# Top-k masks computed between projection tiles, output transposes one place later, one convolution tap on ScalarE

## The reference

```python
gdn_out = gdn_mixer(g_qkv, ...)      # gated delta rule, chunks of 64, 4 heads; output normed and gated
att = dsa_attend(...)                # scores of an indexer, the top 256 (or T // 4) keys of a query, softmax over them
ssm_out = ssd_mixer(s_z, s_xbc, ...) # state space scan
x = x + gate1 * (concat([gdn_out, att, ssm_out]) @ w_out)
```

```python
y = sum(ext[:, j:j + T] * w[j] for j in range(4))
_, sel = lax.top_k(score, topk)      # ties to the lower index
o = o * rsqrt(mean(o * o) + EPS) * norm_g * silu(gate)
```

## Time and profile before

| | |
|---|---|
| median of 3 runs | 4491.47 us (4491.46 to 4493.82) |
| profiled execution, its own time | 4497.23 us |
| its span | 4495.4 us |
| mean granted TensorE clock | 0.947 |
| TensorE busy, share of the span | 91% |
| VectorE, ScalarE | 50%, 23% |

### The profile page before, as it was taken

One profiled execution on the slowest core, in us unless ns is written; L12 is line 12 of the kernel. 1 busy time (PEld: TensorE's weight loads), 2 busy tenths in 40 slices (PEclk: granted clock), 3 DMA queues, 4 the chain that ended last, 5 costly groups with the idle time before them and its releaser, 6 DMA issues.

```text
span 4495.4 us, 54493 instructions
## 1 busy us (share of the span) xinstructions
PE 4086.0 (91%) x21348; PEld 2293.8 (51%) x21348; DVE 2255.5 (50%) x4568; ACT 1029.1 (23%) x2145; POOL 68.8 (2%) x128
## 2 busy tenths in 40 slices
PE   5999888688989999999989998977889799999996
PEld 2545554457545555545545455544575455554553
DVE  3246566655344445454542565565562444444445
ACT  2134444234210000000021344442350100000001
POOL 0000000000000000000000000000000000000000
PEclk8999999789989999999999999987999899999998
DMA  4124111123121322121121121111231111111211
GB/s 196 47 101 149 45 50 38 62 100 123 34 86 66 113 97 92 38 80 38 39 92 58 44 69 50 56 65 57 83 120 40 70 41 45 38 38 38 80 33 56
DMA packets 112880, 311.28 MB, mean 69 GB/s; under 512 B 9456, under 2 KB 57264, under 8 KB 104816
## 3 DMA queue, kind: packets, MB, share of 16 engines
q1 hardware_dynamic: 101392, 253.06, 16.2%
q0 software_dynamic: 10368, 40.58, 2.3%
q10 hardware_dynamic: 864, 14.16, 0.7%
HBM read 253.03 MB, written 54.47 MB: 68 GB/s over the span
## 4 chain that ended last, share of the span: by engine, by line
PE 83%; DVE 8%; DVEq 3%; ACT 2%; issue 2%; ACTq 1%; DMA 1%; SPq 0%; POOL 0%; POOLq 0%
PE PS L1287 34%; PE PS L803 15%; PE PS L1280 6%; PE PS L1328 3%; PE PS L783 2%; DVE big L1793 2%; DVE hT L1793 2%; PE PS L1364 2%; PE PS L1216 2%; PE PS L905 1%; PE PS L731 1%; PE PS L1236 1%; PE PS L970 1%; DVE big L1790 1%; PE PS L981 1%
## 5 line engine op out<-in xcount | busy, mean ns | idle before, releaser
L803 PE MATMUL PS<-hT,ring 128*128 128x512 f32 (+1 forms) x2304 | 844.6, 512 | 0.0
L803 PEld LDWEIGHTS PS<-hT,ring 128*128 128x128 f32 x2304 | 372.5, 196 | 318.3 <-issue 306.8
L1287 PE MATMUL PS<-hT,ring 128*128 128x512 f32 x832 | 372.4, 600 | 16.8 <-ACTq L1430 10.4
L1287 PE MATMUL PS<-xT 128*128 128x512 f32 x704 | 314.7, 601 | 24.2 <-DVEq L2500 24.2
L1287 PE MATMUL PS<-hT,xT 128*128 128x512 f32 x704 | 310.5, 594 | 0.0
L1287 PEld LDWEIGHTS PS<-hT,ring 128*128 128x128 f32 x832 | 159.1, 193 | 221.4 <-issue 220.9
L1280 PE MATMUL PS<-big,ring 128*128 128x512 f32 (+1 forms) x768 | 252.6, 489 | 0.0
L1545 ACT ACTIVATE big<-xT,tk 128x896 bf16<-128x896 f32 (+2 forms) x192 | 231.7, 1207 | 51.5 <-DVEq L1966 44.0
L1287 PEld LDWEIGHTS PS<-xT 128*128 128x128 f32 x704 | 135.8, 193 | 196.3 <-issue 196.3
L1949 DVE TENSOR_SCALAR_CACHE_REDUCE big<-xT,tk 128x384 bf16<-128x384 f32 (+5 forms) x262 | 215.1, 821 | 26.5 <-issue 1.3
L1397 ACT ACTIVATE big<-big 128x1152 f32<-128x1152 f32 x72 | 83.8, 1164 | 559.5 <-DVEq L2633 544.9
(11 more groups left out here) (374 smaller groups left out, 5351.5 us busy)
## 6 DMA issues: line engine op xcount, KB each, us to landing
big<-in_w_ada SPq DMA_DIRECT2D x80, 512.0 KB, 6.2
ring<-in_w_in SPq DMA_DIRECT2D x54, 512.0 KB, 3.5
scr<-big POOLq DMA_DIRECT2D x40, 576.0 KB, 3.1
ring<-in_w_gate SPq DMA_DIRECT2D x44, 512.0 KB, 3.6
ring<-in_w_up SPq DMA_DIRECT2D x44, 512.0 KB, 4.5
hT<-in_kcache SPq DMA_DIRECT2D x16, 1024.0 KB, 6.2
hT<-in_vcache SPq DMA_DIRECT2D x16, 1024.0 KB, 6.9
ring<-in_w_down SPq DMA_DIRECT2D x32, 512.0 KB, 4.2
```

Source lines behind the costliest of these rows:

```text
L803: x = mm(PS[:, o:o + m], w[:, k, :], hT[:, k, c0:c0 + m], start=(k == 0), stop=(k == KT - 1))
L1287: i = mm(bank(b), w[:, k, :], x[:, k, :], start=(k == 0), stop=(k == n - 1))
```

## The change

The lane M goes. Its work becomes the end of the search lane B, two hops a mask (the first joined to the hop that fixes the thresholds), so that it stands between projection tiles and delta-rule hops, in the order of blocks 0 to 6, with one signal at the end; its scratch moves out of the weight ring. The search has 40 hops beside the early tiles where it had 27. The empty projection places after the last tile go from 7 to 2. The transposes of the delta rule's output move: of a pair's first tile behind the `z` products, of its second into the next pair's first hop, behind the row sums; the hop of its own goes, and waits for `oe` (VectorE has written the output and read the banks) stand where the transposes stood. The tap on the newest position is made by ScalarE at the eviction, from PSUM, with the bias, and VectorE makes the other three. SyncE loads one output weight more among the tiles. The lists are now D with A and B (61, 25, 40), D with G and B (110, 92, 71), G with T (32, 36).

```diff
+D_TAIL = 2
-MASK_TILES = (2, 3, "s", 4, 5, 6, 7)
-MASK_ORDER = tuple(6 if _t == "s" else _t - PT0 for _t in MASK_TILES)
-MASK_HOPS = (0, 0, 1, 1, 3, 3, 4, 4, 5, 5, 6, 6, 7, 7, 8, 8) + tuple(range(10, 14)) + tuple(range(16, 20)) + tuple(range(22, 26))
...
+        scan = big[:, o_cs2 + 520:o_cs2 + 1560]
...
-        mask_ready = signal("mask_ready", 7)
+        mask_ready = signal("mask_ready", 1)
...
-        G_HOPS = 4 * (5 + 10 + 12 + 1) + (5 + 6 + 5)
+        G_HOPS = 4 * (5 + 10 + 12) + (5 + 6 + 5)
...
-        B_HOPS = 3 * 32 + 2
-        D_HOPS = ND * DH + 7
+        B_HOPS = 3 * 32 + 1 + 14
+        D_HOPS = ND * DH + D_TAIL
...
-        B_A = 27
-        G_D = 96
+        B_A = 40
+        G_D = 92
         order = weave(D=DH) + weave(D=I_HOPS, I=I_HOPS) + weave(D=D_I, A=A_HOPS, B=B_A) + \
-            weave(D=D_HOPS - D_A, G=G_D, B=B_HOPS - B_A) + masked(weave(G=G_HOPS - G_D, T=T_HOPS)) + weave(S=S_HOPS)
+            weave(D=D_HOPS - D_A, G=G_D, B=B_HOPS - B_A) + weave(G=G_HOPS - G_D, T=T_HOPS) + weave(S=S_HOPS)
...
-                            if h == 1 and i + 6 < NPROJ + 2:
+                            if h == 1:
                                 load_pos(i + 6)
                             yield
-                    for h in range(7):
+                    load_pos(ND + 6)
+                    for h in range(D_TAIL):
                         yield
...
-                sp.wait_ge(*mask_ready.at(l, 7))
-                for n in range(NPROJ + 2, NPROJ + KT):
+                for n in range(NPROJ + 4, NPROJ + KT):
                     load_pos(n)
...
                         if q:
-                            pe.wait_ge(*g["out"].at(l, 2 * q))
+                            pe.wait_ge(*g["oe"].at(l, 2 * q))
...
                         i.then_inc(*g["row"].up())
+                        if q:
+                            turn_out(PAIRS[q - 1][1])
                         yield
                         pe.wait_ge(*g["sq"].at(l, q + 1))
+                        if q:
+                            pe.wait_ge(*g["out"].at(l, 2 * q))
...
                                 if p == 1 and c == 0:
-                                    turn_out(pair[0])
+                                    pe.wait_ge(*g["oe"].at(l, t))
...
                                 i.then_inc(*g["z"].up())
+                                if p == 1 and c == 0:
+                                    turn_out(pair[0])
                                 yield
...
-                        turn_out(pair[1])
-                        yield
...
-                        if t in MASK_TILES and hp == 0 and c == 0:
-                            pe.wait_ge(*mask_ready.at(l, 1 + MASK_TILES.index(t)))
+                        if t == PT0 and hp == 0:
+                            pe.wait_ge(*mask_ready.at(l, 1))
...
+                    if kind == "conv":
+                        if c == 0:
+                            if tile_kind(D_TILES[i - 2]) == "rot":
+                                sc.wait_ge(*rotated.at(l, i + 2))
+                            sc.wait_ge(*act_stored[i % 2].at(l, stores_before(i)))
+                        q = D_TILES[i] - LEAD
+                        act_(dst, src, ACT.Copy)
+                        act_(cout[i % 2][:, c0:c0 + m], PS[:, o:o + m], ACT.Identity, scale=par[:, P_CW + q * 4 + 3:P_CW + q * 4 + 4],
+                             bias=par[:, P_CB + q:P_CB + q + 1])
+                        dr().then_inc(*proj_evac.up())
+                        return
...
                     as_float(FB, T)
-                    yield
-                def masks_dve():
-                    dv.wait_ge(*proj_done.at(l, 3 + 3 * ND))
-                    for j in MASK_ORDER:
+                    for j in range(7):
...
-                        V.tensor_scalar(sel[:, 0:n], sco, thr, None, ALU.is_equal)
+                        V.tensor_scalar(sel_any[:, 0:n], sco, thr, None, ALU.is_equal)
                         dr()
-                        yield
...
-                        dr().then_inc(*mask_ready.up())
+                            dr().then_inc(*mask_ready.up())
+                        dr()
                         yield
...
-                            if kind == "conv" and 1 <= h <= 4:
+                            if kind == "conv" and 1 <= h <= 3:
                                 conv_tap(D_TILES[j], e, c, h - 1)
-                            if kind == "conv" and h == 5:
+                            if kind == "conv" and h == 4:
                                 conv_tail(D_TILES[j], e)
...
-                    if j == 0:
-                        bb = par[:, P_CB + q:P_CB + q + 1]
-                        V.tensor_scalar(cs[:, 0:TPR], ext[e][:, 0:TPR], w, bb, ALU.mult, ALU.add)
-                        V.tensor_scalar(smp(cs), es[:, :, 0:TS], w, bb, ALU.mult, ALU.add)
-                    else:
-                        stt(cs[:, 0:TPR], ext[e][:, j:j + TPR], w, cs[:, 0:TPR], ALU.mult, ALU.add)
-                        stt(smp(cs), es[:, :, j:j + TS], w, smp(cs), ALU.mult, ALU.add)
-                    if j < 3:
+                    stt(cs[:, 0:TPR], ext[e][:, j:j + TPR], w, cs[:, 0:TPR], ALU.mult, ALU.add)
+                    stt(smp(cs), es[:, :, j:j + TS], w, smp(cs), ALU.mult, ALU.add)
+                    if j < 2:
...
+                def gate_out(t, gate, b0):
+                    stt(mixT[:, 0:2, t * 128:(t + 1) * 128], PS[:, b0:b0 + 256].rearrange("p (h t) -> p h t", h=2),
+                        par[:, P_GNG:P_GNG + 1], gate, ALU.mult, ALU.mult).then_inc(*g["out"].up())
...
+                        if q:
+                            dv.wait_ge(*g["ot"].at(l, 2 * q))
+                            dv.wait_ge(*gg_in[(q - 1) % 2][1].at(l, (q - 1) // 2 + 1))
+                            gate_out(2 * q - 1, glg[(q - 1) % 2][1], 768)
                         yield
...
-                                if p == 1 and c == 0:
-                                    dv.wait_ge(*g["ot"].at(l, t))
-                                    dv.wait_ge(*gg_in[q % 2][0].at(l, q // 2 + 1))
-                                    gate_out(pair[0], 0, 768)
                                 yield
                                 dv.wait_ge(*g["z"].at(l, ch))
...
                                 yield
+                                if p == 1 and c == 0:
+                                    dv.wait_ge(*g["ot"].at(l, t))
+                                    dv.wait_ge(*gg_in[q % 2][0].at(l, q // 2 + 1))
+                                    gate_out(pair[0], glg[q % 2][0], 768)
                                 dv.wait_ge(*g["su"].at(l, ch))
...
-                        dv.wait_ge(*g["ot"].at(l, pair[1] + 1))
-                        dv.wait_ge(*gg_in[q % 2][1].at(l, q // 2 + 1))
-                        gate_out(pair[1], 1, 768)
                         if q == 3:
                             dr().then_inc(*s_final.up())
-                        yield
```

More of the change, by code:

```diff
@@ L631, in gdn_sp @@
                                 load_q(t, p)
-                        for i in range(24 if q < 4 else 12):
+                        for i in range(23 if q < 4 else 12):
                             yield
@@ L910, in _, with turn_out @@
                         rotate(2, 0, 0)
+                def turn_out(t):
+                    pe.wait_ge(*g["on"].at(l, t + 1))
+                    ot = gbuf[0]["ot"].rearrange("p h v -> p (h v)")
+                    for hp in range(2):
+                        i = nc.tensor.transpose(PS[:, 768 + hp * 128:896 + hp * 128], ot[:, hp * 128:(hp + 1) * 128], ident)
+                    i.then_inc(*g["ot"].up())
                 def gdn_pe():
@@ L987, in gdn_pe @@
                             break
-                        def turn_out(t):
-                            pe.wait_ge(*g["on"].at(l, t + 1))
-                            ot = d["ot"].rearrange("p h v -> p (h v)")
-                            for hp in range(2):
-                                i = nc.tensor.transpose(PS[:, 768 + hp * 128:896 + hp * 128], ot[:, hp * 128:(hp + 1) * 128],
-                                                        ident)
-                            i.then_inc(*g["ot"].up())
                         for p, t in enumerate(pair):
@@ L1520, in proj_act @@
                     for i in range(ND + 1):
-                        for h in range(DH if i < ND else 7):
+                        for h in range(DH if i < ND else D_TAIL):
                             if i == 0 and h == 0:
@@ L1554, in bisect_act @@
                         yield
-                    yield
+                    for i in range(14):
+                        yield
                 def gdn_act():
@@ L2049, in masks_dve @@
                         yield
[L2050 removed]
+                        stt(scan[:, 0:n], scan[:, 0:n], NEED[:, j:j + 1], sel_any[:, 0:n], ALU.is_le, ALU.mult)
                         dr()
[L2052 to L2053 removed]
+                        stt(sel_any[:, 0:n], sco, thr, scan[:, 0:n], ALU.is_gt, ALU.add)
```

(6 more changed lines are left out.)

24 lines of the change are left out of this document (3 added, 21 removed).

## The result

The changed kernel takes 4364.1 us (median of 4 runs, 4355.3 to 4368.2) against 4492.65 us in the same comparison: a ratio of 0.971, 95% interval 0.969 to 0.973, so 128.5 us faster. The forecast was 4438, with a range from 4400. The direction was right; the gain is more than twice the 54 us forecast, and outside the range.

What follows compares the result with a forecast made beforehand. TensorE's program order was taken as the spine, so only its idle time counts; terms -56 - 8 + 25 - 20 + 5 + 0 = -54 from 4497.2 gave 4443 profiled, 4438 us median, with a range of 4410 to 4465 (4400 to 4482 with rivals).

Steps and rivals of the forecast that it cites:

- the waits of attention: Attention stretch: with the masks gone, 28 of 40.6 us of TensorE waits a layer go, -56 in all.
- the price of the masks between the tiles: Turn stretch: thresholds and masks there raise TensorE's idle time, +12.6 us a layer, +25 in all.
- Attention's clock: Attention stretch: the granted clock partly recovers, taking 4 us of busy TensorE a layer, -8 in all.
- The output's turns: Delta-rule output transposes, pairs 0 and 1: shorter waits and less lower-clock time, 10 us a layer, -20 in all.
- The walk through the turn: Turn stretch, hop by hop: VectorE becomes the bound, TensorE idle 42 us against 29, +12.6 a layer.
- the shorter tail: Five empty tail places go: counted inside the walk; 5 us a layer if VectorE were not the bound there.
- The rival worked out beside the Trainium skill: Turn: long waits from the masks each paid twice through the throttled clock, 8 us a layer more, 4454; no chance given.
- Early search and tap: Early search: 40 hops instead of 27 cost 2.5 us a layer, +5; fourth tap moved to ScalarE, 0.
- The first (new waits as dear as the old): Turn: masks between tiles cost as much as they free, slower, +15 (4506) to +62 at worst; chance 0.10.
- The second: Attention keeps its length, ScalarE's exponentials and copies replacing the shares; -10, 4481; chance 0.14.
- The third: Early search chokes as VectorE's lag passes its slack, 15 us more a layer; -24, 4467; chance 0.12.
- The fourth: Turn costs nothing net and the clock recovers fully; -91, 4400; chance 0.14.

Runs made afterwards that it cites:

- c_many: Changed kernel plus 36 mask-free VectorE maxima, three in each of 12 softmax shares of attention; ratio 0.9962.
- c_few: Changed kernel plus the same 36 VectorE maxima, twelve in each of three softmax shares of attention; ratio 0.9918.
- a_nomask: Changed kernel with the masks' VectorE instructions replaced by memsets to zero at their places between the tiles; 4339 us, ratio 0.9657.
- b_masks: Kernel before with only the masks moved between the tiles, with their weight loads; ratio 0.9780.
- a_tail7: Changed kernel with seven empty tail places again instead of two; ratio 0.9732.
- b_tail2: Kernel before with only the empty tail places cut from seven to two; ratio 0.9952.
- a_early27: Changed kernel with 27 hops of the search early instead of 40; ratio 0.9745.
- b_masks_turns: Kernel before with the masks and the output's turns moved, tail, early search and tap as before; 4379 us, ratio 0.9746.

## Why the prediction was wrong in size

By stretch and layer, the early search was forecast at +2.5 and measured +3; from pair 0's row sums to the first exponentials the forecast was +2.6 (turns -10, masks +12.6) and the measurement -16.5; attention was forecast at -32 and measured -48. So the miss has two halves of some 19 and 16 us a layer. The direction, the waits of attention and the price of the masks between the tiles were right, and not by luck.

**Attention's clock, the first step that failed.** "186 us of busy TensorE at 0.90 would be 176 ... I take 4 of those 10." Measured: 16.7 a layer, so 33 and not 8. The term was made from the mean clock of a window. The same prediction had nearly the right price, 1.6 us at the lower level for a wait, from the earlier trace rows, and used it for the turns alone. In layer 1's attention, from the first logits, the waits of over 2.1 us fell from 13 to 4, and the spells at the lower level from 12 to 3. Nine times 1.6 is 14, and at the 2 us or so of c_many and c_few it is 18; the busy time of that window fell by 18.2 (195.8 to 177.7). The waits themselves (-28) were right: -29.8.

**The output's turns, the second.** "Pairs 0 and 1 have two of each ... Pair 2 is inside the turn, already counted": 10 a layer, with the lower level charged for two waits of four. By itself the edit gives 26 a layer and saves in all six places. Not all six waits were 3.8 us: the second of pair 1 was 2.43. The second turn of a pair was given 0.7 us; it waits 2.42, 1.14 and 1.15 where it waited 3.71, 2.43 and 3.80, so it gains 1.3 to 2.7. The first waits 0.52 and 0.60 in pairs 0 and 1, better than the 1.0 worked out. Taken out of the full change the turns are worth 15 a layer; added to the masks alone, 8.

**The walk through the turn.** It gave 42 us of idle time against 29, and the windows show 31.6 against 28.5, with three projection places more inside. The wait behind thresholds and mask 0, forecast at 9.7, is there: 8.84 (below). The price of the masks was right too, 11.7 a layer by a_nomask and 10 by b_masks. Wrong was "VectorE becomes the bound of this stretch", and with it that the turns of pair 2 and the shorter tail are worth nothing there. VectorE is busy 79 of 103 us. The two turns (7.6 us of waits became 1.2) and the tail (some 5 a layer by a_tail7, 11 by b_tail2) can pay most of the masks' price back; no run isolates this in the turn stretch.

```profile
2865.72 1.11 PE L1006 MATMUL PS<-big 64*64 64x64 f32 x8 [8.84 <-DVE big L1794]
2866.76 0.69 PE L906 MATMUL PS<-cf,big 128*128 128x128 f32 x2
2867.25 5.19 PE L793 MATMUL PS<-hT,ring 128*128 128x512 f32 x8
```

That wait is paid twice as well (5.19 us where eight such matmuls took 3.70 earlier), and so is the one of 4.74 us at line 971 (5.63 us for the eight behind it). The rival worked out beside the Trainium skill, TensorE: Matmul & The Clock Gate, at 4454, therefore held at these waits. It pointed the wrong way because I set it against the new waits and not against those that left.

**Early search and tap.** +5 and 0 were forecast; undone, they cost 16 and 12. The cost side was right: 3.0 us a layer against 2.5, VectorE busy 88 of 113 us (its three taps of a tile are 4.9 us by the earlier trace rows, not 5.9, which changes nothing in the sum). Left out was the other side, 19 us of VectorE work that no longer stand between the delta rule's steps (a_early27's woven and turn stretch is 6.4 us longer with them), and the tap's.

**The sum.** The terms do not add. Masks and turns and tail alone make 172, the whole change 131. Taken out one by one its parts make 141, which these intervals cannot tell from 131. Waits for VectorE take one another's place.

**The rivals.** The first (new waits as dear as the old) is excluded by b_masks; its place and its wait were real, its price was not reached. The second is excluded by attention's 47 us. The third did not come at 40 hops; at 46 it begins, with 4.4 us of waits a layer where it had 15. The fourth came nearest: at the turn nearly nothing net, and most of the clock back. It stood at 4400 and had the turns at the recorded 10 a layer.

Left open: which of the solve's waits each of the five parts moves in the woven stretch. The totals are shown; that VectorE's order is the reason for the overlap is argued from b_masks_turns' waits, not isolated.

## What to carry to other kernels

Count the waits of TensorE that a change removes, and charge each with its length and with the matmuls behind it at the lower level (here about 2 us for each wait of 3 us or more); a mean clock of a window hides this. Before busy times of two traces are compared, compare their counts of matmuls. Work that must stall TensorE cost less in three long pieces than in twelve short ones, by 10 us a layer here (247.5 against 257.6). Where an engine is busy three quarters of a stretch, do not price relief for it at nothing, and do not add such terms: test them from both ends, alone and taken back out.

## What was not expected of the hardware

A wait of 13.7 us left the next eight matmuls no slower (2.07 us) than one of 3.8 did (2.08). Three long waits, 37 us of added idle time, added 6.6 us of matmul time; the lengthened waits of twelve shares, 32 us of added idle time, added 21.8.

Shorter waits can cost the same, but do not always. In the kernel before the granted clock fell during a wait of 1.84 us (at 3127.65; one of 1.56 us had ended 4 us before it began); in the change one of 2.22 us (at 3066.45) left it at the higher level. One row misleads here:

```profile
3017.79 2.08 PE L1209 MATMUL PS<-big 128*128 128x128 f32 x8 [2.12 <-DVE big L2408]
```

In c_many these eight matmuls too took 2.08 us, but the clock was at the lower level from 3013.0 on, before this wait of 2.12 us began, so the row says nothing of what such a wait costs.
